# Inverse of the delta matrices: who empties the powers and the sums, and how the blocks are turned

## The reference, cut to what matters

```
M     = strict(beta * decay * (K @ K.T))      # 128 x 128, one per chunk, direction and head
inv   = inverse(I + M)                        # used as  v_new = inv @ (beta * (v - decay * (K @ state)))
```

## Time and profile before

| | us |
|---|---|
| median of 3 runs | 2599.92 |
| lowest and highest | 2597.69, 2603.49 |
| the profiled execution | 2606.47 |
| its span | 2604.3 |

### The profile page before, as it was taken

How to read it: one execution, slowest core, us unless ns; L and a number is a source line. 1 busy time by engine, 2 the same in 40 slices (tenths; PEclk the granted TensorE clock), 3 DMA queues, 4 the chain that set the end, 5 groups by cost and what they waited for, 6 DMA issues and landing times. The chain is left out here.

```text
span 2604.3 us, 41857 instructions
## 1 busy us (share of the span) xinstructions
PE 2137.1 (82%) x16766; PEld 1888.2 (73%) x16766; DVE 1735.9 (67%) x2872; ACT 915.0 (35%) x1253; POOL 128.9 (5%) x111
## 2 busy tenths in 40 slices
PE   5938669988556996987797887689977899999997
PEld 2938459978446995874677776689975677899996
DVE  2663768876766875663275686458999677666665
ACT  1300534333243343323123413344456333444443
POOL 1000000000000000530000050000000000000000
PEclk9955889998778998996659988899999999999998
DMA  5726158838025871311000001457610666555553
GB/s 189 265 37 166 47 219 314 315 138 288 7 98 201 312 288 48 118 47 65 3 0 4 5 1 74 170 157 228 216 48 0 204 214 209 208 192 186 186 190 142
DMA packets 167336, 377.47 MB, mean 145 GB/s; under 512 B 12522, under 2 KB 111594, under 8 KB 154986
## 3 DMA queue, kind: packets, MB, share of 16 engines
q1 hardware_dynamic: 157794, 365.48, 40.9%
q10 hardware_dynamic: 9360, 9.44, 1.0%
HBM read 363.87 MB, written 11.01 MB: 144 GB/s over the span
## 5 line engine op out<-in xcount | busy, mean ns | idle before, releaser
L1136 DVE TENSOR_TENSOR experts_v_lo<-experts_v,experts_v_hi 128x1024 fp32r<-128x1024 f32 x128 | 156.9, 1225 | 98.5 <-ACT experts_v_hi L1110 97.7
L1084 PE MATMUL experts_py<-experts_v_hi,experts_c_hi 128*128 128x512 f32 x512 | 204.7, 400 | 19.7 <-DVE experts_v_lo L1136 19.2
L1291 PE MATMUL ffn_pa<-all_h_hi,ffn_u_hi 128*128 128x256 f32 x704 | 198.8, 282 | 21.5 <-DVE ffn_u_lo L1350 21.5
L1110 ACT CAST experts_v_hi<-experts_v 128x1024 fp32r<-128x1024 f32 x128 | 134.8, 1053 | 221.3 <-PE experts_py L1088 112.6
L1085 PE MATMUL experts_py<-experts_v_lo,experts_c_hi 128*128 128x512 f32 x512 | 201.9, 394 | 0.0
L1292 PE MATMUL ffn_pa<-all_h_lo,ffn_u_hi 128*128 128x256 f32 x704 | 198.3, 282 | 0.0
L1293 PE MATMUL ffn_pa<-all_h_hi,ffn_u_lo 128*128 128x256 f32 x704 | 198.1, 281 | 0.0
L1088 PE MATMUL experts_py<-experts_v_hi,experts_c_lo 128*128 128x512 f32 x512 | 158.9, 392 | 0.0
L2656 PE MATMUL route_pa<-all_h_hi,route_u_hi 128*128 128x256 f32 x512 | 146.4, 286 | 8.9 <-DVE route_u_lo L2541 8.9
L1291 PEld LDWEIGHTS ffn_pa<-all_h_hi,ffn_u_hi 128*128 128x128 f32 x704 | 134.4, 191 | 23.7 <-DVE ffn_u_lo L1350 22.2
L1070 PE MATMUL experts_pa<-all_h_hi,experts_u_hi 128*128 128x256 f32 x512 | 144.7, 283 | 1.5 <-DVE experts_u_lo L1131 1.5
(11 more groups left out here) (554 smaller groups left out, 6012.1 us busy)
## 6 DMA issues: line engine op xcount, KB each, us to landing
experts_v<-in_peer_v SPq DMA_DIRECT2D x128, 512.0 KB, 3.4
ffn_u<-in_ffn_columns SPq DMA_DIRECT2D x44, 1024.0 KB, 8.4
ffn_ada_w<-in_ada_w SPq DMA_DIRECT2D x36, 1024.0 KB, 5.8
route_u<-in_peer_u SPq DMA_DIRECT2D x64, 512.0 KB, 3.8
experts_u<-in_peer_u SPq DMA_DIRECT2D x64, 512.0 KB, 4.4
ffn_v<-in_ffn_rows SPq DMA_DIRECT2D x44, 512.0 KB, 8.5
proj_ada_w<-in_ada_w SPq DMA_DIRECT2D x12, 1024.0 KB, 5.6
proj_w<-in_diff_w_in SPq DMA_DIRECT2D x12, 1024.0 KB, 6.6
```

Of the source, the lines that this page charges most:

```text
L1084: pe.matmul(py[:, 2 * t + n, :], c_hi[:, b, part], v_hi[:, b, cols], start=start, stop=False)
L1136: dve.tensor_tensor(v_lo[:, i % 2, :], v[:, i % 2, :], v_hi[:, i % 2, :].bitcast(F32), ALU.subtract).then_inc(v_split, 1)
L1291: pe.matmul(out, u_hi[:, b, cols], h_hi[:, c, :], start=(c == 0), stop=False)
```

## The change

- The turn is done by quarters: 24 products of 64 x 64 with the identity `eye`, for each head the two quarters on the diagonal and the one off it, in place of 8 transposes of 128 x 128. ScalarE copies them in three instructions: Y in two parts into `xy`, and the quarter off the diagonal into the new `y_off`.
- ScalarE copies all powers out of `pxy`, now also in phase 4. `xy` has two buffers, one for the odd and one for the even phases.
- VectorE adds the identity to Y for heads 4 to 7 only, and out of `xy` in SBUF, not out of `pxy`. For heads 0 to 3 `apply` multiplies by Y itself, and VectorE adds the old `s` to the sum as it moves it out of `psum`. For heads 4 to 7 it copies the sum, as before.
- In phase 5 VectorE writes heads 0 to 3 back to `at_m` and ScalarE heads 4 to 7, each in two instructions.
- The first `s` is made by GpSimd, into a tensor of its own, `s_first`, in two subtractions for each chunk and direction. It runs ahead of the other engines by up to one chunk.
- The semaphores are split: `copied` becomes `y_ready`, `off_ready`, `xy_ready`, `vt_ready` and `own_ready`; `squared` becomes `turned`, `squared` and `crossed`; `s_ready` and `xy_ready` count per half of the heads.

The diff, cut to its core:

```diff
-        y_full = st.sb("y_full", [P, 2, DN_HEADS, P])
-        xy = st.sb("xy", [P, 2, DN_HEADS, 2, BLK])
-        yi = st.sb("yi", [P, 2, 2, DN_HEADS, BLK])
+        y_off = st.sb("y_off", [P, DN_HEADS, BLK])
+        xy = st.sb("xy", [P, 2, 2, DN_HEADS, 2, BLK])
+        yi = st.sb("yi", [P, 2, 2, 4, BLK])
+        s_first = st.sb("s_first", [P, 2, DN_HEADS, BLK])
...
+            def turn(d, g):
+                own, other = halves[d], halves[1 - d]
+                m = at_m[:, g, d]
+                for head in range(DN_HEADS):
+                    cols = slice(head * BLK, (head + 1) * BLK)
+                    for half in halves:
+                        pe.matmul(powers(d)[half, head, 0, :], m[half, head, half], eye[half], start=True, stop=True)
+                    last = pe.matmul(psum[other, d, 1, cols], m[own, head, other], eye[own], start=True, stop=True)
+                last.then_inc(turned[d], 1)
...
             def square(d, g, step):
-                pe.wait_ge(copied[d], 11 * g + 1 + 2 * step)
-                if step:
-                    pe.wait_ge(yi_ready[d], 10 * g + 2 * step)
+                if step == 0:
+                    pe.wait_ge(y_ready[d], 2 * g + 2)
+                else:
+                    both(xy_ready[d], 5 * g + step)
...
             def apply(d, g, step):
-                pe.wait_ge(yi_ready[d], 10 * g + 2 * step)
-                pe.wait_ge(s_ready[d], 6 * g + step)
-                if step == 1 and g:
-                    pe.wait_ge(inverse_ready[d], g)
+                pe.wait_ge(xy_ready[d][0], 5 * g + step)
+                pe.wait_ge(yi_ready[d], 5 * g + step)
+                if step == 1:
+                    pe.wait_ge(off_ready[d], g + 1)
+                    pe.wait_ge(first_ready[d], 2 * g + 2)
+                    if g:
+                        pe.wait_ge(inverse_ready[d], g)
+                else:
+                    both(s_ready[d], 4 * g + step - 1)
...
+                        y = yi[src, last % 2, d, h, :] if head >= 4 else xy[src, last % 2, d, head, 1, :]
...
-                        last = pe.transpose(pxy[:, d, h // 4, h % 4 * P:(h % 4 + 1) * P], m[:, h, :], k["ident"][:])
...
+        @block.gpsimd
+        def _(pool):
+            pool.wait_ge(eye_ready, 1)
+            for g in range(TILES):
+                for d in range(2):
+                    if g:
+                        pool.wait_ge(applied[d], 5 * g - 4)
+                        pool.wait_ge(s_ready[d][0], 4 * g - 3)
+                    for half in halves:
+                        pool.tensor_tensor(s_first[half, d], eye[half].unsqueeze(1).broadcast_to([BLK, DN_HEADS, BLK]),
+                                           at_m[half, g, d, :, half], ALU.subtract).then_inc(first_ready[d], 1)
...
         @block.scalar
-                    act.copy(y_full[:, d], pxy[:, d].rearrange("p m (h n) -> p (m h) n", h=4)).then_inc(copied[d], 1)
+                    for heads in (slice(0, 4), slice(4, 8)):
+                        act.copy(xy[:, 1, d, heads, 1], powers(d)[:, heads, 0]).then_inc(y_ready[d], 1)
+                    act.copy(y_off[other], psum[other, d, 1, :].rearrange("p (h n) -> p h n", h=DN_HEADS)
+                             ).then_inc(off_ready[d], 1)
...
+                    if phase < levels:
+                        act.wait_ge(squared[d], 5 * g + phase + 1)
+                        if phase >= 2:
+                            act.wait_ge(applied[d], 5 * g + phase - 1)
+                        elif g:
+                            act.wait_ge(applied[d], 5 * g)
+                        parts = slice(0, 2) if phase < levels - 1 else slice(1, 2)
+                        act.copy(xy[:, phase % 2, d, 0:4, parts], powers(d)[:, 0:4, parts]).then_inc(xy_ready[d][0], 1)
+                        act.copy(xy[:, phase % 2, d, 4:8, parts], powers(d)[:, 4:8, parts]).then_inc(xy_ready[d][1], 1)
+                    if phase == levels:
+                        act.wait_ge(applied[d], 5 * g + levels)
+                        for half in halves:
+                            act.copy(m[half, 4:8, half], sums(d)[half, 1]).then_inc(own_ready[d][1], 1)
...
         @block.vector
+                    if phase < levels:
+                        dve.wait_ge(xy_ready[d][1], 5 * g + phase + 1)
...
+                        dve.tensor_tensor(yi[:, phase % 2, d], xy[:, phase % 2, d, 4:8, 1, :], wide_eye, ALU.add
+                                          ).then_inc(yi_ready[d], 1)
...
+                    if 1 <= phase < levels:
+                        dve.wait_ge(applied[d], 5 * g + phase)
+                        dve.tensor_tensor(s[:, d, 0:4], sums(d)[:, 0], before[:, d, 0:4], ALU.add
+                                          ).then_inc(s_ready[d][0], 1)
+                        dve.tensor_copy(s[:, d, 4:8], sums(d)[:, 1]).then_inc(s_ready[d][1], 1)
+                    if phase == levels:
+                        dve.wait_ge(applied[d], 5 * g + levels)
                         for half in halves:
+                            dve.tensor_tensor(m[half, 0:4, half], sums(d)[half, 0], s[half, d, 0:4], ALU.add
+                                              ).then_inc(own_ready[d][0], 1)
```

More of the change, by code:

```diff
@@ L2024, in _, with blocks, both @@
         def _(pe):
-            def blocks(step):
-                for h in range(4):
-                    for head in (h, h + 4):
-                        for b in range(2):
-                            flips = step - 1 if head >= 4 and 1 <= step <= 4 else 0
-                            turns = 1 if head >= 4 and 1 <= step <= 4 else 0
-                            yield head, (b + flips) % 2, (b + flips + turns) % 2
+            def blocks(step, h):
+                for head in (h, h + 4):
+                    for b in range(2):
+                        flips = step - 1 if head >= 4 and 1 <= step <= 4 else 0
+                        turns = 1 if head >= 4 and 1 <= step <= 4 else 0
+                        yield head, (b + flips) % 2, (b + flips + turns) % 2
+            def both(sems, n):
+                for sem in sems:
+                    pe.wait_ge(sem, n)
+            def turn(d, g):
[7 more added lines that the diff above has]
+                last.then_inc(turned[d], 1)
             def square(d, g, step):
@@ L2036, in square @@
                 m = at_m[:, g, d]
-                pe.wait_ge(copied[d], 11 * g + 1 + 2 * step)
-                if step:
-                    pe.wait_ge(yi_ready[d], 10 * g + 2 * step)
-                for head, a, b in blocks(step):
-                    src, dst = halves[a], halves[b]
-                    if step == 0:
-                        x, y = m[src, head, src], y_full[src, d, head, src]
-                    else:
-                        x, y = xy[src, d, head, 0, :], xy[src, d, head, 1, :]
-                    if step < levels - 1:
-                        pe.matmul(out[dst, head, 0, :], y, x, start=True, stop=True)
-                    last = pe.matmul(out[dst, head, 1, :], x, y, start=True, stop=True)
+                if step == 0:
+                    pe.wait_ge(y_ready[d], 2 * g + 2)
+                else:
+                    both(xy_ready[d], 5 * g + step)
@@ new lines, in square @@
+                for h in range(4):
+                    for head, a, b in blocks(step, h):
+                        src, dst = halves[a], halves[b]
+                        if step == 0:
+                            x, y = m[src, head, src], xy[src, 1, d, head, 1, :]
+                        else:
+                            x, y = (xy[src, (step - 1) % 2, d, head, i, :] for i in range(2))
+                        if step < levels - 1:
+                            pe.matmul(out[dst, head, 0, :], y, x, start=True, stop=True)
+                        last = pe.matmul(out[dst, head, 1, :], x, y, start=True, stop=True)
@@ L2049, in square @@
                 last.then_inc(squared[d], 1)
             def apply(d, g, step):
-                pe.wait_ge(yi_ready[d], 10 * g + 2 * step)
-                pe.wait_ge(s_ready[d], 6 * g + step)
-                if step == 1 and g:
-                    pe.wait_ge(inverse_ready[d], g)
-                for head, a, b in blocks(step):
-                    src, dst = halves[a], halves[b]
-                    last = pe.matmul(sums(d)[dst, head // 4, head % 4, :], yi[src, d, step % 2, head, :],
-                                     s[src, d, head, :], start=True, stop=True)
@@ new lines, in apply @@
+                last = step - 1
+                for h in range(4):
+                    for head, a, b in blocks(step, h):
+                        src, dst = halves[a], halves[b]
+                        y = yi[src, last % 2, d, h, :] if head >= 4 else xy[src, last % 2, d, head, 1, :]
+                        done = pe.matmul(sums(d)[dst, head // 4, head % 4, :], y, source[src, d, head, :], start=True,
+                                         stop=True)
+                done.then_inc(applied[d], 1)
@@ new lines, in _ @@
```

(7 more changed lines are left out.)

73 lines of the change are left out of this document (26 added, 47 removed).

## The result

| | before | changed |
|---|---|---|
| median of 6 runs each, taken together | 2601.24 us | 2612.59 us |
| lowest and highest | 2594.38, 2605.14 | 2608.07, 2616.14 |
| ratio, with its 95% interval | | 1.0051 (1.0034 to 1.0068) |
| the profiled execution | 2606.47 | 2614.32 |

The changed kernel is slower: by 11.35 us between the medians (0.44%), by 0.51% in the ratio. The forecast was slower too, but by 6.2 us, at 2606.1, and 2612.5 was the upper end of its range: the time lies 0.1 us beyond it. Of the 6.5 us between forecast and time, 1.3 are a shift in the median of before, which was 2599.92 when the forecast was made and is 2601.24 in the series above.

The account below looks back on a forecast made before the run. The inverse stage was taken as bound by TensorE's instruction count, in blocks of 256. 1373.2 + 33 x 3.80 + 8.75 ends it at 1507.4, +6.2 us, so a median of 2606.1 us; range 2597 to 2612.5.

Parts of the forecast that it names:

- The bound: Inverse stage: bound by the number of TensorE instructions, streamed in blocks of 256, about 3.8 us each.
- Engines decide: Inverse stage: blocks are hidden; only the shorter turn counts against the later s, at most -2.4 us, 2597.5; 0.08 with rival 5.
- The count: TensorE's program in the stage: +90 instructions for each of 8 turns, +720, from 8152 to 8872.
- rival 5: In the turn, identity products go as one record: +42 instead of +90, about +1 us, 2601; 0.08 with Engines decide.
- The first block end: Early in the stage: the first block end moves from 1376.69 to about 1373.2, 57 instructions into the first square.
- The time of a block, c: Inverse stage: 256 TensorE instructions take 3.80 us, for 33 blocks from the first block end; break-even at 3.61.
- Rivals 1 and 2: Inverse stage: blocks get shorter; c 3.45 to 3.76, likeliest 2601, chance 0.31; or c below 3.45, 2593, chance 0.11.
- The rest behind the last block end: Stage's end, last square and apply of the last tile: 8.75 us, against 8.8 before.
- Nothing outside the stage changes: Rest of the kernel: no change but where blocks begin; over 2 us there would be a surprise.
- Busy times: Inverse stage after the change: VectorE busy some 55 us, ScalarE some 60.
- shared port: Inverse stage: GpSimd's subtractions hold up VectorE's two-SBUF-input additions, up to +4.8 us on top, 2611; chance 0.08.
- Rival 4: The shared port: 16 GpSimd subtractions each hold one VectorE addition, an apply late by 0.3 us, +4.8 us; chance 0.08.

Follow-up runs that it names:

- quarter turn alone: Kernel before with only the turn changed: 24 products with the identity for 8 transposes, and the copies they need; ratio to before 1.0024, stage 138.1 us.
- wide turn put back: Changed kernel with the turn as before: 8 transposes of 128x128 and three copies on ScalarE; 2602.63 us against 2598.79, ratio 1.0021, stage 136.0 us.
- where the blocks begin: Changed kernel with 32 one-column products (128 instructions, half a block) once ahead of the first turn; ratio to before 1.0051, stage 144.1 us.
- first s on VectorE: Changed kernel with the first s made by VectorE and no GpSimd in the stage; ratio to before 1.0041, stage 140.0 us.
- count alone: Kernel before with 20 unread one-column products ahead of each turn, 80 instructions more per turn; ratio to before 1.0038, stage 143.9 us.
- two operations doubled: Changed kernel with ScalarE's first copy of the powers and VectorE's addition of the identity each done twice; ratio to before 1.0080, stage 153.3 us.
- fewer products: Changed kernel's plan with the wide turn and, for heads 0 to 3, shared 128-column products in phases 1 to 3; ratio to before 1.0030, stage 138.8 us.

## Why the prediction was too small, and what was right in it

The mechanism was right: TensorE's instructions, by blocks of 256, set the middle. What failed are terms of the sum: the block time carried into the lone start, the duration of the tail carried over from before, and the split of the semaphores, which was put at nothing.

**The bound.** Right: the number of TensorE's instructions, in blocks of 256, sets the middle of the stage. The quarter turn alone costs it 7.1 us with TensorE less busy, the wide turn put back gives it back, and 256 instructions take 3.75 to 3.88 us in the middle of eleven executions. "Engines decide", for which the prediction named the Trainium skill, "Runtime: NRT & Kernel Launch", section "Instruction fetch mechanics", with its "mostly hidden", is out: 29 of the stage's 34 block ends have gaps of over 0.25 us, 32.1 us in all (24 of 32, and 20.8 us, in before).

**The count.** Nearly right. 8872 were forecast, 8832 came: +640 from the turns as said, but only five more separate waits for a tile and direction, not ten. The packets agree (34 or 35 forecast), as does the product's form, which settles rival 5: L2049 has 256 loads for 128 in the code. The DMA queue (packets, MB, share), and the loads of the new turn:

```profile
q8 instruction: 34, 0.56, 1.6%
```

```profile
L2049 PEld LDWEIGHTS dninv_pxy<-dninv_eye,dna_at_m x256: 129/135/223, 1364.2 to 1479.1; 64*64 64x64 f32 x128
```

**The first block end.** Right: forecast 4.7 us behind the stage's start, measured 4.46.

**The time of a block, c.** Right where both directions run, wrong where one is alone. The three executions have 3.93, 3.79 and 3.88 over their 33 blocks, mean 3.866, against 3.80 taken: 33 x 0.066 = +2.2 us. But the middle has 3.88, 3.75 and 3.83, mean 3.82, and only +0.6 us of the 2.2 lies there. +1.2 lies in the lone start behind the first block end, where 2.6 blocks took 11.0, 10.9 and 10.9 us and not 9.8. There the chain of engines sets the time: all 3.1 us of waiting for ScalarE's first copy (L2154) lie in it, and no unnamed gap but one, and in its first part the granted clock was still 0.50. The sum had let blocks count from the first block end on. (+0.4 lies between the tail's start and the last block end.) Rivals 1 and 2, by which denser work makes blocks faster, are not borne out: before had 3.84 to 3.87 in its middle, mean 3.85, and the spread is larger than that difference.

**The rest behind the last block end.** This step failed: 8.75 us were carried over from before, and it took 10.76, 10.12 and 10.89, +1.85 on average. The end of the stage, in before (10 us), in the wide turn put back (the last 4), and in the changed kernel (parts of the last 12):

```profile
1491.20:1501.20 10.00, 5.18 (x166) 4.46 (x158) 4.93 (x9) 2.19 (x4) 0.00 (x0) 1.00 0.01 2
```

```profile
1498.67:1500.67 2.00, 1.11 (x17) 0.95 (x14) 0.69 (x1) 0.58 (x1) 0.00 (x0) 0.50 0.00 0
1500.67:1502.67 2.00, 1.26 (x12) 1.07 (x11) 0.69 (x1) 0.00 (x0) 0.00 (x0) 0.50 0.00 0
```

```profile
1496.80:1498.80 2.00, 1.27 (x64) 1.06 (x59) 0.81 (x3) 0.45 (x2) 0.00 (x0) 1.00 0.00 0
1498.80:1500.80 2.00, 0.71 (x23) 0.60 (x15) 1.09 (x3) 0.20 (x1) 0.00 (x0) 0.83 0.00 0
1500.80:1502.80 2.00, 1.44 (x28) 1.25 (x24) 0.42 (x2) 0.50 (x2) 0.00 (x0) 0.50 0.04 8
...
1506.80:1508.80 2.00, 1.28 (x13) 1.09 (x11) 0.68 (x1) 0.00 (x0) 0.00 (x0) 0.50 0.00 0
```

Before ran all of its tail at a granted clock of 1.00, which is 2.4 GHz; the changed kernel ran most of it at 0.50, 1.2 GHz. What a product costs more there is seen on the last instruction of the stage, VectorE's L2127 before and L2175 now, which waits for the same eight products of the merge: 1.30 us before, 2.12 us now.

```profile
1508.12 0.69 DVE L2175 TENSOR_SCALAR dna_at_m<-dninv_psum 64x512 f32<-64x512 f32 x1 [2.12 <-PE dninv_psum L2110]
```

The granted clock of each execution's tail, read from the trace: when it fell from 1.00 to 0.50 for good, and how much of the tail lies behind the fall (us):

| execution | fell | stage ended | tail behind the fall | tail |
|---|---|---|---|---|
| before, first | 1501.35 | 1501.16 | none | 8.65 |
| before, second | 1497.58 | 1496.29 | none | 8.57 |
| before, third | 1501.44 | 1500.30 | none | 8.58 |
| quarter turn alone | 1505.38 | 1507.30 | 1.9 | 8.91 |
| where the blocks begin | 1500.64 | 1505.29 | 4.6 | 10.35 |
| changed, second | 1497.55 | 1504.65 | 7.1 | 11.29 |
| first s on VectorE | 1497.90 | 1505.13 | 7.2 | 11.35 |
| count alone | 1504.29 | 1512.20 | 7.9 | 11.15 |
| changed, first | 1500.11 | 1508.81 | 8.7 | 12.21 |
| wide turn put back | 1492.49 | 1502.67 | 10.2 | 11.64 |
| two operations doubled | 1510.06 | 1520.46 | 10.4 | 12.61 |
| changed, third | 1501.56 | 1512.11 | 10.5 | 12.33 |

The more of the tail lies behind the fall, the longer it is, by about a third of a microsecond for each. (The first execution of the changed kernel, the count alone and the two operations doubled had the clock back at 0.50 for 3.4 to 10.2 us in between as well.) In before the clock fell as well, but 0.2, 1.3 and 1.1 us behind the end of the stage. Two windows of before, on both sides of it:

```profile
1500.00:1501.15 1.15, 0.43 (x8) 0.29 (x5) 0.69 (x1) 0.00 (x0) 0.00 (x0) 1.00 0.00 0
1501.36:1502.50 1.14, 0.00 (x0) 0.00 (x0) 0.00 (x0) 0.00 (x0) 0.00 (x0) 0.50 0.05 14
```

So before escaped the fall narrowly. Why it comes when it comes stays open: from the clock's rise to its fall it was 126.3 us in all three executions of before and in the second and third of the changed kernel, but 112.6 to 136.5 in the others, and whether a longer stage merely met the fall, or its own thin stretches brought it, these runs don't part. Ahead of the fall TensorE worked for 0.71 of 2 us, but before, with 0.75 at the leanest, kept its clock. The fall comes inside the tail with the count alone too, whose ScalarE, VectorE and tail are those of before: it is no matter of their share, and the tail's 2.5 us there don't come from a later s.

**"Nothing outside the stage changes."** This failed by 1.4 us. At a stage's end GpSimd clears the stage's semaphores one by one (`Stage.clear`) before it goes on; the change splits 17 into 37. The first GpSimd instruction of the next stage, changed kernel:

```profile
1511.72 1.81 POOL L2298 MEMSET dnrec_state<- 128x2048 f32 x1 [52.79 <-issue]
```

and before:

```profile
1502.64 1.81 POOL L2248 MEMSET dnrec_state<- 128x2048 f32 x1 [216.59 <-issue]
```

They come 2.90 and 1.49 us behind the end of their stages. All kernels lie on one line: 17 semaphores 1.49 us (four profiles), 19 semaphores 1.63, 37 semaphores 2.90 (six), 39 semaphores 3.04 and 3.05 (two operations doubled, fewer products). That is 0.07 us for each, with the work before it very different, so I call it shown. It is on the path: TensorE's first load of the next stage comes 5.09 us behind the stage's end in before and 6.51 in the changed kernel, later by the same 1.4. The prediction listed the split of the semaphores and gave it no price.

**Busy times and the shared port.** VectorE 58.3 (some 55 forecast), ScalarE 58.8 (some 60): right. Rival 4 took place as a mechanism, in three additions of 40, and cost nothing that I could see.

**The sum again**, in means: forecast +6.2; a block's time +2.2; the rest behind the last block +1.85; the first block end -0.2; the semaphores +1.4. That is +11.45, against +11.35 by the medians of the first series. That they agree within 0.1 us is luck: the sum goes by the first profile of before, whose stage is 0.7 us over the mean of its three (with the mean it is 12.1), and the ratio of both series, 1.0051, is 13.3 us. Split the other way, by the runs: the turn costs 6.2 (put in alone) to 6.6 us (taken out, against the mean), which is what had been forecast for the whole. The run without the new turn is slower than before by 1.0021, or 5.5 us (1.8 to 9.1), of which its stage has 4.1 and the semaphores 1.4. That 4.1 is the other parts of the change together with this run's own copies and clock; what each has of it wasn't measured.

## What to carry to other kernels

Where TensorE waits for nothing that has a name, inside runs of equal small products, count its instructions: a change that shortens other engines' work there buys nothing, and one that cuts a product into quarters pays by the instruction even if TensorE itself gets less busy. To tell such a limit from others, look at where the gaps stand in the count, and shift the program by half a block. Price what stands beside the work too: each semaphore of a stage is cleared at its end. And don't carry the duration of a lone tail over without looking when the clock falls: before, it fell 0.2 to 1.3 us behind the end, and in the nine executions of the other kernels in the table it fell inside the tail.

## What the runs showed of the hardware that was not expected

- About 3.8 us for a block of 256 instructions is a floor that doesn't move with density: 3.84 to 3.87 in the middle before, 3.75 to 3.88 after and in the other runs that keep the products. What sets it wasn't found. Where TensorE's instructions are longer (fewer products, 4.3 us for 256 in the middle) it isn't seen at all.
- 0.07 us of GpSimd for each semaphore that is cleared, the same from 17 to 39 of them, and the next stage's first load waits for it.
- A granted clock that holds at 1.00 through 8.6 us of thin work in three executions of one kernel and falls to 0.50 just behind it, 0.2 to 1.3 us, and that falls 1.9 to 10.5 us ahead of the end of nearly the same work in nine executions of others.
- An addition on VectorE with two SBUF inputs that begins inside a subtraction on GpSimd ends 0.28 us behind it (0.50, 0.92 and 1.27 us in place of 0.43), while a copy out of PSUM isn't held up. The Trainium skill, "SBUF — State Buffer", section "SBUF: two separate sides", has this as the lock between the two, and these traces agree.
